# Decayed attention products of six levels, cut into two column groups of 64 keys by 64 queries

## What is computed

```python
cum = jnp.cumsum(g, axis=-2)                      # g: per-channel log decay, <= 0
pair = jnp.where(lower[..., None],
                 jnp.exp(jnp.minimum(c_i[..., :, None, :] - c_i[..., None, :, :], 0.0)), 0.0)
a_i = jnp.einsum('bhid,bhjd,bhijd->bhij', q_i, k_i, pair)
o_i = jnp.einsum('bhij,bhjv->bhiv', a_i, v_i) + jnp.einsum('bhid,bhdv->bhiv', qd_i, S)
```

## Time and profile before

| | us |
|---|---|
| median of 3 runs | 1687.05 |
| lowest and highest of them | 1686.17, 1687.37 |
| the profiled execution | 1686.5 |
| its span in the trace | 1684.8 |

### The profile page before, as it was taken

One profiled execution on the slowest core, in us unless ns is written; L12 is line 12 of the kernel. 1 busy time (PEld: TensorE's weight loads), 2 busy tenths in 40 slices (PEclk: granted clock), 3 DMA queues, 4 the chain that ended last, 5 costly groups with the idle time before them and its releaser, 6 DMA issues.

```text
span 1684.8 us, 21675 instructions
## 1 busy us (share of the span) xinstructions
PE 1673.5 (99%) x7752; PEld 1391.4 (83%) x7752; DVE 1030.8 (61%) x1152; ACT 805.8 (48%) x976; POOL 54.7 (3%) x83
## 2 busy tenths in 40 slices
PE   9999999999999999999999999999999999999997
PEld 7888888888888888888888888888888888888886
DVE  5544466565887888765555546556555455465765
ACT  5544454443567554665444344444443443444653
POOL 7000000000000000000000000000000000000001
PEclk9999999999999999999999999999999999999999
DMA  8666655666576555547666666666666666666563
GB/s 272 181 184 186 189 163 163 209 239 208 154 248 178 148 165 160 152 136 249 190 186 189 197 188 187 192 191 190 188 190 194 187 188 196 189 187 189 175 196 128
DMA packets 159135, 315.87 MB, mean 187 GB/s; under 512 B 9728, under 2 KB 9728, under 8 KB 158176
## 3 DMA queue, kind: packets, MB, share of 16 engines
q1 hardware_dynamic: 157456, 304.12, 59.8%
q0 software_dynamic: 1616, 10.87, 1.8%
HBM read 310.77 MB, written 4.19 MB: 187 GB/s over the span
## 4 chain that ended last, share of the span: by engine, by line
PE 97%; DVE 1%; DMA 1%; issue 1%; ACT 0%; POOLq 0%; POOL 0%; DVEq 0%; SPq 0%; ACTq 0%
PE acc L594 30%; PE acc L596 30%; PE acc L595 30%; PE aux L610 2%; PE aux L762 2%; DMA w_raw<-in_gla_w_in 1%; PE aux L618 0%; PE aux L663 0%; DVE w_lo L1302 0%; PE aux L773 0%; PE aux L775 0%; PE aux L774 0%; PE acc L628 0%; PE acc L631 0%; PE acc L634 0%
## 5 line engine op out<-in xcount | busy, mean ns | idle before, releaser
L1302 DVE TENSOR_TENSOR w_lo<-w_raw,w_hi 128x1024 fp32r<-128x1024 f32 x572 | 702.2, 1230 | 569.5 <-ACT w_hi L956 568.7
L956 ACT CAST w_hi<-w_raw 128x1024 fp32r<-128x1024 f32 x572 | 600.9, 1051 | 824.6 <-PE acc L596 801.0
L594 PE MATMUL acc<-w_hi,a_hi 128*128 128x512 f32 x1648 | 648.7, 394 | 0.0
L596 PE MATMUL acc<-w_hi,a_lo 128*128 128x512 f32 x1648 | 642.1, 390 | 0.0
L595 PE MATMUL acc<-w_lo,a_hi 128*128 128x512 f32 x1648 | 641.6, 389 | 0.0
L596 PEld LDWEIGHTS acc<-w_hi,a_lo 128*128 128x128 f32 x1648 | 309.3, 188 | 65.0
L594 PEld LDWEIGHTS acc<-w_hi,a_hi 128*128 128x128 f32 x1648 | 309.5, 188 | 62.3 <-issue 0.3
L595 PEld LDWEIGHTS acc<-w_lo,a_hi 128*128 128x128 f32 x1648 | 309.7, 188 | 62.1
L594 PE MATMUL acc<-w_hi,act_hi 128*128 128x512 f32 x320 | 124.6, 389 | 0.0
L596 PE MATMUL acc<-w_hi,act_lo 128*128 128x512 f32 x320 | 124.5, 389 | 0.0
L595 PE MATMUL acc<-w_lo,act_hi 128*128 128x512 f32 x320 | 124.5, 389 | 0.0
(11 more groups left out here) (251 smaller groups left out, 860.5 us busy)
## 6 DMA issues: line engine op xcount, KB each, us to landing
w_raw<-in_ffn_w_in SPq DMA_DIRECT2D x176, 512.0 KB, 3.7
w_raw<-in_w_in SPq DMA_DIRECT2D x112, 512.0 KB, 4.0
w_raw<-in_gla_w_in SPq DMA_DIRECT2D x96, 512.0 KB, 3.7
w_raw<-in_ffn_w_out SPq DMA_DIRECT2D x88, 512.0 KB, 3.8
w_raw<-in_w_out SPq DMA_DIRECT2D x32, 512.0 KB, 4.5
w_raw<-in_gla_w_out SPq DMA_DIRECT2D x32, 512.0 KB, 4.3
w_raw<-in_ple_w_gate SPq DMA_DIRECT2D x32, 512.0 KB, 4.6
x_raw<-in_x_cols SPq DMA_DIRECT2D x8, 256.0 KB, 6.1
```

The lines of the kernel that those rows point to most:

```text
L594: pe.matmul(banks[t][:], hi[:, k + c, tok], wh, start=st, stop=False)
L596: mm = pe.matmul(banks[t][:], lo[:, k + c, tok], wh, start=False, stop=en)
L956: nc.scalar.copy(w_hi[u % RING][:], w_raw[u % RING][:]).then_inc(hi_done, 1)
L1302: nc.vector.tensor_tensor(w_lo[u % RING][:], w_raw[u % RING][:], w_hi[u % RING][:], ALU.subtract).then_inc(lo_done, 1)
```

## The change

In the levels with 2h <= 64 (h = 1, 2, 4, 8, 16, 32), each product of 128 keys by 128 queries becomes two products of 64 keys by 64 queries, the first with tokens 0 to 63 of the 128-token half, the second with tokens 64 to 127. The first writes partitions 0 to 63 of the bank, the second partitions 64 to 127, each at the columns of its own queries. Since the output's first partition sets the column group of the array, the built program has the first with a tile of 128 rows by 64 columns at column 0, the second with the same tile at column 64. The two groups take turns inside the loop over `kb`. The two squares off the diagonal are not computed, and keep what the bank held; the masks of these levels leave them out. Levels 64 and 128 are as before. Nothing else changes, on no other engine.

```diff
+GROUP = 64
...
                 for c in range(2 * TT):
                     hd, t = 2 * pair + c // TT, c % TT
 
+                    if 2 * h <= GROUP:
+
+                        for kb in range(2):
+                            for r in range(0, P, GROUP):
+                                tok = slice(t * P + r, t * P + r + GROUP)
+                                mm = pe.matmul(b[r:r + GROUP, c * P + r:c * P + r + GROUP], keys[:, 2 * hd + kb, tok],
+                                               queries[:, 2 * hd + kb, tok], start=kb == 0, stop=kb == 1)
+                        continue
                     q = 1 - t if h == P else t
                     for kb in range(2):
                         mm = pe.matmul(b[:, c * P:(c + 1) * P], keys[:, 2 * hd + kb, t * P:(t + 1) * P],
```

## The result

| | us |
|---|---|
| before, median of 5 runs | 1687.05 (1686.14 to 1687.37) |
| changed, median of 5 runs | 1678.26 (1677.84 to 1678.38) |
| ratio, with its 95% interval | 0.995 (0.9939 to 0.9961) |
| the profiled execution, its span | 1677.84, 1676.1 |

A forecast was written before the change was run, and what follows sets the result against it. TensorE was taken to bound the kernel. Six levels gaining 1.63 us each gave 9.8, with 0 for width changes and VectorE: 1686.5 - 9.8 = 1676.7 profiled, median 0.5 above, 1677.3 us; range 1676 to 1692.

The forecast's parts named there:

- TensorE bounds, and what its stream loses, the kernel loses: Whole kernel: TensorE is busy for 99% of the span, so any change in its program's length is paid in full.
- Do the groups work at the same time?: Six changed levels: if not, +0.4 us in all; if so in loads and matmuls, 9.8 us gained.
- The likeliest case: Six changed levels: both column groups work at once, a product pair every 78 ns or less; 1676.3 to 1681 us, chance 0.38.
- the other cases: Changed levels: partial overlap 1683 to 1685 us, 0.08; groups alternating 1687 to 1690, 0.29; minimum record spacing 1690.5 to 1696, 0.25.
- The argument for turns: Changed levels: a load starts only when the record before starts, so matmuls never overlap; 1687 to 1690 us, chance 0.29.
- The slot: Changed levels: time for one record of each group side by side, 61 ns; 32 make a level of 1.95 us.
- The floor: Changed levels: groups alternate and records cannot start every 57 ns, only every 65 to 78; 1690.5 to 1696 us, chance 0.25.
- Switching between widths: Into and out of the six levels, twelve changes between full-width products and narrower tiles: booked at 0, at most 0.1 us.
- that rule: The Trainium skill's drain at tiling-mode changes: twelve changes at about 0.17 us each, some 2 us; not booked.
- The sum: Six changed levels: each 1.95 us instead of 3.58, a gain of 1.63, 9.8 us in all.
- VectorE keeps up: Level's period of 18.3 us after the change: VectorE busy for 17.2, 1.1 spare, so 0 booked for it.
- its wait for the second step: VectorE's idle time of 0.68 us in a level's period, expected to go with faster steps.

The follow-up runs named there:

- the thin product: Changed kernel with the thin low-rank product (32 products of 64 and 32 weight columns) read as plain instead of rounded float32: 1692.36 us.
- runs of eight: Changed kernel with eight records of one column group, then eight of the other, instead of alternating record by record: 1681.87 us.
- runs of four: Changed kernel with four records of one column group, then four of the other, instead of alternating record by record: 1678.37 us.
- runs of sixteen: Changed kernel with all sixteen records of a step's first column group, then all of the second's: 1686.09 us, ratio 0.9999 to the kernel before.

## Why the prediction was right, point by point

- **TensorE bounds, and what its stream loses, the kernel loses.** Right: every run's time followed from the length of its levels (in one run, of the thin product) within the scatter of the start, with 3.85 us a level at the slow end and 1.50 at the fast one.
- **Do the groups work at the same time?** The likeliest case was the true one, with 0.38. The trace of before could not settle it, and the range, 1676 to 1692, held most of the other cases too: that the time lies in it says little. Three runs show the mechanism: the order alone takes the gain away, leaving one group out gives nothing, and four groups give more. The argument for turns, that a load never started before the record ahead, was a property of products that share columns: with two groups, loads start 7 ns apart.
- **The slot.** Taken as 61 ns between 57 and 65; measured 58. The floor had 0.25 on the strength of the earlier trace rows, and those rows were misread. The two records' own starts are 59 ns apart for the loads and 84 for the matmuls, not 65 and 78 (which came from a merged row's rounded length). So even this pair showed no floor of 65 for a load, and its 84 stands right behind a switch (next point), where the second record of a group comes late: 107 ns instead of 58 with one group alone.
- **Switching between widths: the step that was mis-sized.** Booked at nothing from the earlier trace rows; it is 0.36 us for each level, 2.1 us in all. That row was read rightly, but its products are rounded float32, and float32 behaves otherwise. The Trainium skill (TensorEngine Tiling (Array Packing), Key Properties) says that a change of tiling mode drains TensorE, and my estimate by that rule was 2 us; for float32 the trace agrees, for rounded float32 it does not. I had written the rule off by a row of another type. The right row was there, among those for the floor. The small product of the earlier trace rows is float32 in less than the whole array (8 of the rows), and this is the timeline of PE around it in the kernel before:

```profile
67.84 0.39 PE L596 MATMUL acc<-w_hi,a_lo 128*128 128x512 f32 x1
...
68.37 0.50 PE L594 MATMUL acc<-w_hi,a_hi 128*128 128x512 f32 x1
...
68.71 0.40 PE L595 MATMUL acc<-w_lo,a_hi 128*128 128x512 f32 x1
```

It starts 0.32 us after the unit product, not 0.23, and its load stopped for 0.35 us with "issue" as the reason. Both stand at every changed level, and neither at a level of before. Its place in the stream is 68.71 - 0.227 - (67.84 + 0.227) = 0.42 us for two records that move 8 columns, so most of it is such a price. Booked for six levels, that would have been some 2 us, as the rule said.

- **The sum.** A level was to be 1.95 us and is 2.21: 0.1 less for the slot and 0.36 more for the ends. The gain was to be 9.8 and is 8.2 by the levels, 8.8 between the medians, the difference being mainly the start. That the forecast is only 1 us off is luck in part: the slot's error and the start's scatter both went against the error of 2.1 us at the ends. By the levels alone the time would have been 1678.9.
- **VectorE keeps up.** Right. Busy 16.9 of 18.4 us, and its wait for the second step is gone.

## What to carry to other kernels

Where a float32 product's mask leaves only blocks on (or beside) the diagonal, cut it into column groups with their own moving columns and alternate the groups record by record or at most in short runs; the time is then that of one group. This was measured for two groups of 64 and four of 32, all in float32. Do it in few, long stretches, as each entry and exit together cost a third of a microsecond here. A row that is to bound a cost must match in data type too, not only in shape and place.

## What the runs showed of the hardware that I had not expected

- Four column groups of 32 run side by side at 81% of the ideal pace: a load and a matmul of 32 float32 columns every 9.2 ns on average over 128 records.
- A matmul can start before three earlier ones of another column group: with runs of eight and sixteen the last record of a level's first step is the 35th to start, not the 32nd. So runs of four cost hardly more than single turns (2.26 against 2.21 us), runs of eight lose nearly half of the gain (2.82), and runs of sixteen nearly all (3.54, against 3.58 before).
- A change of width costs 0.13 us within a stream of float32 products and 0.36 us for a whole excursion from full-width rounded float32 and back; between rounded float32 products of 128, 64 and 32 columns it costs nothing that shows.
- Halving the weight columns alone, with all moving columns kept, gains nothing (3.85 us against 3.58).
